# A two-layer hybrid transformer block on one core: one 512-column matmul on a constant in each pair of heads of the context queries' attention

## The reference

```python
def token_mixer(h, hc, p, rope_hd, rope_mla, with_ctx_out):
    ...
    outs.append(blocked_attend(q, jnp.concatenate([k, kc], axis=1), jnp.concatenate([v, vc], axis=1)))
    if with_ctx_out:
        outs_c.append(softmax_attend(qc, kc, vc, None))
...
    for l in range(DEPTH):
        last = l == DEPTH - 1
        ...
        y, yc = token_mixer(h, hc, p, rope_hd, rope_mla, not last)
        x = x + gt1 * rms_norm(y, g_post_mix[l])
```

## Time and profile before

| | |
|---|---|
| Runs | 2521.42 us median of 3 (2516.55 to 2522.45) |
| The profiled execution's own time | 2520.4 us |
| Its span in the trace | 2518.6 us |
| PE busy | 2287.4 us (91%) |
| DVE, ACT, POOL busy | 1011.7, 678.4, 810.1 us |
| Mean granted TensorE clock | 0.938 |
| Share of PE in the chain that ended last | 81% |

### The profile page before, as it was taken

How to read it: one execution, slowest core, us unless ns; L and a number is a source line. 1 busy time by engine, 2 the same in 40 slices (tenths; PEclk the granted TensorE clock), 3 DMA queues, 4 the chain that set the end, 5 groups by cost and what they waited for, 6 DMA issues and landing times.

```text
span 2518.6 us, 46185 instructions
## 1 busy us (share of the span) xinstructions
PE 2287.4 (91%) x19414; PEld 1836.8 (73%) x19414; DVE 1011.7 (40%) x1473; ACT 678.4 (27%) x1181; POOL 810.1 (32%) x570
## 2 busy tenths in 40 slices
PE   5999899879989799999999699989997888999997
PEld 3888566559967588888888468846667866788885
DVE  3000555564653741414142420055556564632543
ACT  3011355642221211111111220135552222311221
POOL 3342243003122423232232544133303215344444
PEclk8998999978989799999999789899986999999998
DMA  6121032000011021212121423003200011223231
GB/s 247 59 80 52 1 134 100 20 3 3 4 60 42 25 68 59 67 58 67 58 67 58 149 68 107 25 7 127 100 22 2 4 53 50 92 92 100 92 100 59
DMA packets 45402, 162.39 MB, mean 64 GB/s; under 512 B 5504, under 2 KB 5504, under 8 KB 45024
## 3 DMA queue, kind: packets, MB, share of 16 engines
q1 hardware_dynamic: 44480, 157.89, 18.9%
q0 software_dynamic: 800, 2.69, 0.3%
HBM read 158.46 MB, written 2.10 MB: 64 GB/s over the span
## 4 chain that ended last, share of the span: by engine, by line
PE 81%; DVE 10%; ACT 4%; issue 2%; POOL 1%; DMA 1%; SPq 0%; POOLq 0%; ACTq 0%; DVEq 0%
PE ps L1322 77%; PE ps L1564 3%; DVE part_h L980 1%; DVE hT L973 1%; DVE xT L998 1%; POOL flat L518 1%; DVE flat L1306 1%; DMA flat<-wmod_dram 1%; DVE small L1075 1%; DVE flat L996 1%; ACT flat L736 0%; PE ps L1829 0%; ACT flat L754 0%; ACT flat L688 0%; DVE ps L1072 0%
## 5 line engine op out<-in xcount | busy, mean ns | idle before, releaser
L1322 PE MATMUL ps<-part_hi,wparts 128*128 128x512 f32 (+1 forms) x3072 | 815.1, 353 | 26.6 <-DVE part_h L980 7.9
L1322 PEld LDWEIGHTS ps<-part_hi,wparts 128*128 128x128 f32 x3072 | 545.0, 191 | 116.2 <-DVE part_h L980 14.3
L499 POOL TENSOR_TENSOR wparts<-flat,wparts 128x1024 fp32r<-128x1024 f32 x184 | 443.2, 2409 | 543.0 <-ACT wparts L909 537.3
L1322 PE MATMUL ps<-flat 64*64 64x32 f32 (+8 forms) x8812 | 496.4, 266 | 68.5 <-DVE flat L1192 29.8
L1322 PEld LDWEIGHTS ps<-flat 64*64 64x64 f32 (+4 forms) x8812 | 386.1, 149 | 175.1 <-issue 92.4
L1322 PE MATMUL ps<-part_h,wparts 128*128 128x512 f32 (+1 forms) x1344 | 474.6, 353 | 0.0
L1322 PE MATMUL ps<-part_mlp,wparts 128*128 128x512 f32 (+1 forms) x1536 | 418.2, 359 | 10.2 <-DVE part_h L980 10.2
L1322 PE MATMUL ps<-part_lo,wparts 128*128 128x512 f32 x960 | 341.7, 356 | 0.0
L1322 PEld LDWEIGHTS ps<-part_mlp,wparts 128*128 128x128 f32 x1536 | 275.6, 191 | 59.2 <-DVE part_h L980 11.9
L909 ACT ACTIVATE wparts<-flat 128x1024 fp32r<-128x1024 f32 x112 | 118.8, 1061 | 704.1 <-PE ps L1322 704.1
L1322 PEld LDWEIGHTS ps<-part_h,wparts 128*128 128x128 f32 x1344 | 257.9, 192 | 31.9 <-issue 0.2
(11 more groups left out here) (198 smaller groups left out, 2062.7 us busy)
## 6 DMA issues: line engine op xcount, KB each, us to landing
flat<-w_dram SPq DMA_DIRECT2D x128, 512.0 KB, 3.5
flat<-wmod_dram SPq DMA_DIRECT2D x94, 512.0 KB, 5.1
flat<-win_dram SPq DMA_DIRECT2D x40, 512.0 KB, 3.6
flat<-wout_dram SPq DMA_DIRECT2D x16, 512.0 KB, 3.6
xT<-xT_dram SPq DMA_DIRECT2D x8, 384.0 KB, 6.8
flat<-rope_dram SPq DMA_DIRECT2D x2, 1024.0 KB, 5.5
out_dram<-xT SPq DMA_DIRECT2D x8, 256.0 KB, 2.0
flat<-wmask_dram SPq DMA_DIRECT2D x2, 768.0 KB, 6.9
```

Source lines behind the costliest of these rows:

```text
L499: pool.tensor_tensor(wlo[q % 2], src, whi[q % 2], ALU.subtract).then_inc(s_used[q], 1)
L1322: return pe.matmul(out, lhsT, rhs, start=start, stop=stop)
```

## The change

In each pair of heads of a context block, one `keep_clock` matmul is put between `spread_sums(p)` and `turns(2p + 1)`. Its weights are the identity and its moving operand the first 512 columns of `kf`; it writes the PSUM bank from column 3584, which these blocks use for nothing else, and nobody reads the result. It waits for no semaphore and raises none. That is 2 blocks x 6 pairs = 12 matmuls, all in layer 0.

```diff
                             scores((p + 1) % 6, at + (2 * p + 2), i + (asked + (1 if p == 5 else 0)))
                             spread_sums(p)
+                            if not win:
+                                keep_clock(3584, 1)
                             turns(2 * p + 1)
```

## The result

The changed kernel took 2532.23 us in the median of 5 runs (2528.05 to 2533.90), against 2518.81 us (2513.61 to 2522.45) for the kernel before in the same runs. The ratio is 1.0051, with a 95% interval of 1.0037 to 1.0064. The forecast was 2531.5 us, slower. The profiled executions are 2531.73 and 2520.4 us, 11.3 us apart.

A forecast was written before the change was run, and what follows sets the result against it. PE was taken as the bound, busy 91% of the 2518.6 us span. A median of 2521.4 us plus 10.2 for twelve unhidden matmuls gave about 2531.5 us, slower; the range was 2526.5 to 2535.8 us.

The forecast's parts named there:

- Nothing hides it: Context-block pairs: no wait begins ahead of the new matmul and ends behind it, so the fraction hidden is taken as nothing.
- rival C: Context blocks, gap before `output`: the gap takes up part of the cost, up to 5.2 us, giving 2526.4 us; chance 0.05.
- The price: Context blocks, PE's order: each added matmul occupies 2 x 0.427 = 0.853 us, 12 of them 10.24 us.
- another pace between narrow neighbours: Sign of a wrong base: the added matmul steps at a pace other than 0.427 us a record between narrow neighbours.
- Rival D: Context-block pairs: each added matmul occupies its full 1.18 us, 14.2 us in all, giving 2535.6 us; chance 0.06.
- E: Whole kernel: the change does nothing measurable, for instance because the trace misreads its time; 2521.4 us; chance 0.02.
- The clock inside the blocks: Context blocks: the clock is already 1.00, the 2.4 GHz level, so nothing can be gained there.
- No later fall was spared: Behind the context blocks: the clock falls at the same pieces of work, about 10 us after 506 and 582.
- A: 48 two-column records behind the blocks: the clock stays up, giving back about 5.0 us, 2526.6 us; chance 0.05.
- B: Scan's first step: a shifted schedule spares the clock's fall, giving back 9.5 us, 2522.1 us; chance 0.04.
- parallel traces: From the context blocks to the end, the two traces should run parallel, about 10.2 us apart.

## Why the prediction was right

**Nothing hides it: right.** PE's idle time is 6.24 us in either trace, and the gap behind the transposes is there 12 times. The same matmul placed in the gap costs 0.36 us instead of 0.90, and doubling it adds as much again. That rules out rival C.

**The price: right in kind, small by 6%.** The sum had 2 x 0.427 us for each, 10.24 in all. The trace has 10.87, 0.906 for a pair. The missed part is at the entrance: the two records last 1.13 us together, so the second starts 1.13 - 0.59 = 0.54 us behind the first and not 0.427, and what follows the transposes comes a little sooner than before. The steps between matmuls in a row, from which the price was taken, don't have this. It is paid once for a run of such matmuls: two in a pair cost 1.77 us, not 1.81. The prediction had named another pace between narrow neighbours as a sign that its base is wrong; the first step did show one, worth 0.6 us in all, and the base held otherwise. Rival D, 1.18 us each, did not happen, nor did E: the blocks grew, and the interval of the ratio leaves out no change.

**The clock inside the blocks: right.** It is 1.00 in both, so there was nothing to regain.

**No later fall was spared: right, rivals A and B did not occur.** Both falls stand behind the same pieces of work, 10 us later. The experiments bear out the reasons given against A in part: idle time and sparse records stand behind the added matmuls, and filling the idle time alone does not prevent the fall. Rival B's price held too: a scan step at full clock gave back 9.9 us, where 9.5 had been worked out from rows 10. But the rival put it down to a shifted schedule; in the traces it took dense work inside the sparse stretch, which the change does not have. Whether a shift alone can do it now and then is open: one run in ten of the kernel with the three in a row was as short as those with the spread ones.

**The rest of the time.** Of the 11.3 us between the profiled executions, 10.87 lie in the blocks. The prediction's parallel traces hold to about 1 us only: at the end the changed kernel lost another 1.4 us to the clock, as PE's last 16 records ran at 0.50 instead of 1.00 and 0.73, and elsewhere it was about 1 us ahead, which was not traced to a cause. The medians of the first comparison are 13.4 us apart. Before's median was 2518.8 in those 5 runs and 2519.5 to 2521.7 in the later ones of 11 to 19 runs, so the 13.4 is likely a little too much; the interval, 9.3 to 16.1 us, holds both. That the median itself, 2532.23 us, came within 0.7 us of the forecast is luck in part: before's median was 2.6 us lower than the 2521.4 that the sum started from, and the difference 3.2 us larger than its 10.2.

## What to carry to other kernels

A matmul meant to keep TensorE's clock up can pay only where the rows show the clock below 1.00 or about to fall. It costs least between the last instruction that a waiting engine needs from PE and PE's own wait, and nothing if it fits into that wait: in this kernel two transposes decide between 0.90 and 0.36 us, with a wait of 0.43. Look for such places by the granted clock of short stretches, not by idle time: the costliest here had no idle time at all, but 4 us of matmuls with two columns and 20 us of small ones behind. Then place the dense matmuls ahead of and among the sparse ones, and test their number and their places.

## What the hardware showed that was not expected

- A stretch in which PE is busy without pause can still let the clock fall: it fell during 24 records of two columns (3.9 us) in the scan, and the 26.58 us behind them ran at a mean of 0.59 with PE busy for all of it. The Trainium skill's page "TensorE: Matmul & The Clock Gate" ("HAM oscillation") puts the falls that it describes down to PE's idle times between bursts; in and just ahead of these 24 records there was none. The small scan matmuls did not bring the clock down from 1.00 (942 records in 27.87 us), yet after the fall at 582.5 us it stayed at 0.50 until 606.4, with PE busy with them or the two-column ones all the while (before, columns as in rows 2):

```profile
581.00:582.00 1.00, 1.00 (x10) 1.00 (x10) 0.42 (x1) 0.00 (x0) 0.00 (x0) 1.00 0.00 0
583.00:584.00 1.00, 1.00 (x6) 1.00 (x7) 0.00 (x0) 0.00 (x0) 0.00 (x0) 0.50 0.00 0
605.00:606.00 1.00, 1.00 (x14) 1.00 (x12) 0.45 (x1) 0.45 (x1) 0.00 (x0) 0.50 0.00 0
607.00:608.00 1.00, 1.00 (x34) 1.00 (x32) 0.22 (x1) 0.22 (x1) 0.00 (x0) 1.00 0.00 0
```

- Three 512-column matmuls, one ahead of those records and two among them, avoided this in both layers of the profiled run, and all four runs were at least 14 us below before's median. The same three just ahead of them did not, and nine of ten runs took as long as before's. One in the middle did not either, but there the clock fell as soon as it had started.
- A 512-column matmul between narrow neighbours costs 0.06 us more than its step in a row of its like (0.906 against 0.853 us); in bfloat16, with weights of 64 columns, it costs 0.21 us in the same place.
